# Stream cross products on four column groups, with three places for u blocks coming in and two going out

## The reference

```python
att = jnp.einsum('bhld,bhmd->bhlm', q, k) * decay
o = (jnp.einsum('bhlm,bhme->bhle', att, v)
     + jnp.einsum('bhld,bhde->bhle', q, S) * jnp.exp(lg[:, None] * (n + 1.0))[:, :, None])
kw = k * jnp.exp(lg[:, None] * (L - 1.0 - n))[:, :, None]
S_new = jnp.exp(lg * L)[:, None, None] * S + jnp.einsum('bhmd,bhme->bhde', kw, v)
...
x += W_o( sig(g_a) * ConvBranch(h) + sig(g_b) * RetentionBranch(h) ),  h = RMSNorm(x)
x += PEER(RMSNorm(x));   y = RMSNorm_final(x)
```

## Time and profile before

| | |
|---|---|
| three runs | 2183.03, 2184.49, 2186.46 us; median 2184.49 |
| the profiled execution | 2185.89 us, its span 2184.1 us |
| TensorE busy | 2139.8 us (98%) |
| VectorE busy | 1746.6 us (80%) |
| ScalarE, GpSimd busy | 619.3 us (28%), 860.8 us (39%) |
| DMA, mean over the span | 335 GB/s |

### The profile page before, as it was taken

The page is one execution under the profiler, slowest core; times in us unless marked ns, Lnnn a source line. Parts: engine busy times, 40 slices in busy tenths (PEclk is TensorE's granted clock), DMA queues, the critical chain, the costliest instruction groups (busy, mean ns, idle before and its releaser), DMA issues.

```text
span 2184.1 us, 31103 instructions
## 1 busy us (share of the span) xinstructions
PE 2139.8 (98%) x10569; PEld 1706.0 (78%) x10569; DVE 1746.6 (80%) x3270; ACT 619.3 (28%) x1197; POOL 860.8 (39%) x606
## 2 busy tenths in 40 slices
PE   6999999999999999999999999999999999999997
PEld 6999989999998985655565565677767888888886
DVE  2577586676765286898989979999969999999998
ACT  4212213132223111121211211233324444443434
POOL 4222122223333004475685675411145444444440
PEclk9999999999999999999999999999999999999999
DMA  5999999989983458999999999888999999999995
GB/s 191 300 329 308 300 299 330 333 299 326 305 287 136 137 195 336 336 372 412 397 410 412 383 412 412 299 290 298 301 340 411 414 414 413 414 414 414 414 415 202
DMA packets 312713, 732.28 MB, mean 335 GB/s; under 512 B 30208, under 2 KB 162048, under 8 KB 312576
## 3 DMA queue, kind: packets, MB, share of 16 engines
q1 hardware_dynamic: 188352, 436.52, 55.4%
q0 software_dynamic: 73728, 268.47, 31.3%
q10 hardware_dynamic: 50496, 25.59, 3.9%
HBM read 602.46 MB, written 128.00 MB: 334 GB/s over the span
## 4 chain that ended last, share of the span: by engine, by line
PE 61%; DMA 16%; DVE 14%; issue 4%; SPq 2%; ACT 1%; POOL 0%; DVEq 0%; ACTq 0%
PE ps L1833 29%; DMA b<-acts 12%; PE ps L1793 6%; PE ps L1596 6%; PE ps L1595 6%; PE ps L1594 6%; DMA b<-in_u_t 4%; PE ps L1848 4%; DVE b L1463 3%; DVE b L1509 2%; DVE b L1446 1%; DVE b L1515 1%; DVE b L1500 1%; SPq L527 1%; DVE b L1103 1%
## 5 line engine op out<-in xcount | busy, mean ns | idle before, releaser
L1833 PE MATMUL ps<-b,b 128*128 128x384 f32 x2048 | 665.6, 486 | 0.0
L732 POOL DMA_INDIRECT b<-u_rows,b x256 | 362.6, 1416 | 677.9 <-DVE b L1446 489.1
L1833 PEld LDWEIGHTS ps<-b,b 128*128 128x128 f32 x2048 | 386.8, 190 | 263.4
L695 POOL TENSOR_TENSOR b<-b,b 128x1024 fp32r<-128x1024 f32 x80 | 196.8, 2463 | 468.6 <-ACT b L745 464.0
L1463 DVE SCALAR_TENSOR_TENSOR b<-b,b,b 128x1024 f32<-128x1024 f32 x256 | 330.8, 1292 | 49.0 <-ACT b L966 32.6
L1594 PE MATMUL ps<-b,b 128*128 128x320 f32 x1152 | 364.5, 316 | 0.0
L1595 PE MATMUL ps<-b,b 128*128 128x320 f32 x1152 | 357.0, 310 | 0.0
L1596 PE MATMUL ps<-b,b 128*128 128x320 f32 x1152 | 357.0, 310 | 0.0
L732 POOL DMA_INDIRECT b<-in_peer_v,b x256 | 288.8, 1128 | 118.1 <-issue 76.9
L1446 DVE CUSTOM_DVE_ANT_0 b<-b,b 128x1024 f32<-128x1024 f32 x256 | 312.5, 1221 | 25.3 <-DMA b<-u_rows,b 23.8
L1103 DVE STREAM_TRANSPOSE b<-b 128x1024 f32<-128x1024 f32 x128 | 158.0, 1241 | 186.5 <-DMA b<-in_u_t 178.7
(11 more groups left out here) (164 smaller groups left out, 2414.0 us busy)
## 6 DMA issues: line engine op xcount, KB each, us to landing
b<-in_u_t SPq DMA_DIRECT2D x256, 512.0 KB, 6.5
u_rows<-b SPq DMA_DIRECT2D x512, 128.0 KB, 4.4
b<-in_peer_v SPq DMA_DIRECT2D x128, 512.0 KB, 22.1
b<-in_w_in SPq DMA_DIRECT2D x72, 512.0 KB, 6.4
b<-in_wq SPq DMA_DIRECT2D x48, 512.0 KB, 4.4
gates<-b ACTq DMA_DIRECT2D x12, 2048.0 KB, 8.3
b<-gates SPq DMA_DIRECT2D x32, 768.0 KB, 17.4
acts<-b SPq DMA_DIRECT2D x120, 192.0 KB, 7.9
```

The costliest lines, as they stand in the source:

```text
L695: nc.gpsimd.tensor_tensor(lo[u][:, :], raw[:, u, :], hi[u][:, :].bitcast(F32), ALU.subtract).then_inc(lo_ready, 1)
L732: nc.gpsimd.indirect_dma_start(slots[n % SLOTS][:, :], None, u_rows if kind == "u" else v_rows, bass.IndirectOffsetOnAxis(ap=row_id[:, r_ ...
L1833: last = nc.tensor.matmul(ps[:, up_bank(e), 0:TD], w[:, k * P:(k + 1) * P], h2[:, k, SD:T], start=(k == 0), stop=(k == KT - 1))
```

## The change

The cross products of all streams of a head are made in one block (`cross`), right behind the prompt's state at t = 4. The decayed q is now the stationary operand, 32 columns (two streams) at a time, and the state moves through it, 256 columns. The four pairs of streams write to four groups of 32 partitions of half a bank. `qg` is made twice, with zeros where the other stream of the pair stands (`own`), so that the second stream's product adds to the first's. The result has rows for frames; ScalarE copies it (`crow`), and at the end of t = 6 TensorE turns it by a product with the identity that adds to the streams' own attention (`stream_outputs`). ScalarE's root no longer waits for the last stream's state and is taken in two parts.

The places for u blocks are three in and two out, so `turn_in(m)` waits for block m - 3 to be turned, and `turn(m)` for block m - 2 to be stored. The ten turns behind the states of streams 1 to 7 are dealt out as 1, 2, 2, 2, 2, 1, 0 instead of 1, 1, 2, 1, 2, 1, 2; in the last head those behind streams 2 to 7 are 2, 2, 2, 1, 2, 1 instead of 2, 1, 2, 1, 2, 2. Left out below are two places that wait for all stores, now counted over two places.

```diff
--- before.py
+++ after.py
@@ -86,6 +86,7 @@
 TURN_IN = (2, 0, 2, 3, 4, 1, 3, 3)
 PER_HEAD = sum(TURN_IN)
 PER_CONV = 6
+TURNED_BEHIND_STREAM = (1, 2, 2, 2, 2, 1, 0)
 TURNED_GB = 2 + PER_HEAD
 TURNED_CONV = HEADS * PER_HEAD + TURNED_GB
 N_CONV = (NKEY - TURNED_CONV) // PER_CONV
@@ -182,7 +183,8 @@
     l = np.arange(P)[None, :]
     same = (l // STEP == m // STEP) & (l >= m)
     dec_s = np.stack([np.where(same, np.exp(g * np.maximum(l - m, 0)), 0.0) * scale for g in lg], 1)
-    gq = np.stack([np.broadcast_to(np.exp(g * (l % STEP + 1)), (P, P)) for g in lg], 1)
+    own = np.stack([l // STEP % 2 == a for a in range(2)], 1)
+    gq = np.stack([np.broadcast_to(np.exp(g * (l % STEP + 1))[:, None, :] * own, (P, 2, P)) for g in lg], 1)
     kcol = np.zeros((P, HEADS, PT + STREAMS))
     for h, g in enumerate(lg):
         for j in range(PT):
@@ -260,8 +262,8 @@
         wa_lo = [take(base, [P, D], F32R) for _ in range(GROUP)]
         ident = take(base, [P, P], F32)
         ones = take(base, [P, P], F32)
-        u_in = [x[:, i, :] for i in range(2)]
-        u_turned = [x[:, 2 + i, :] for i in range(3)]
+        u_in = [x[:, i, :] for i in range(3)]
+        u_turned = [x[:, 3 + i, :] for i in range(2)]
         g1 = take(base, [P, KT], F32)
         g2 = take(base, [P, KT], F32)
         ss = take(base, [P, TT], F32)
@@ -283,7 +285,7 @@
         sin = take(r, [P, T], F32)
         dec = take(r, [P, PROMPT], F32)
         dec_s = take(r, [P, P], F32)
-        gq = take(r, [P, P], F32)
+        gq = take(r, [P, 2 * P], F32)
         kcol = take(r, [P, HEADS, PT + STREAMS], F32)
         g16 = take(r, [P, HEADS], F32)
         kv = take(r, [P, TT, DK + DV], F32)
@@ -295,7 +297,8 @@
         att_at = [0, 512, 896, 1152, 1280]
         att_n = [512, 384, 256, 128, 128]
 
-        qg = [kv[:, 0, i * P:(i + 1) * P] for i in range(2)]
+        qg = [[kv[:, a, d * P:(d + 1) * P] for d in range(2)] for a in range(2)]
+        crow = att[:, 0:DV]
         sq = [att[:, i * T:(i + 1) * T] for i in range(2)]
         xs = at(conv_from, [P, 2, D], F32)
         hf = at(conv_from + 8192, [P, 2, 512], F32)
@@ -427,7 +430,9 @@
         st_stored = [sem(f"stream_state_stored{i}") for i in range(STREAMS)]
         s_loaded = [sem(f"s_loaded{i}") for i in range(STREAMS)]
         qg_ready = sem("qg_ready")
-        cross_done = sem("cross_done")
+        cross_done = sem("cross_rows_done")
+        crow_ready = sem("cross_rows_ready")
+        streams_done = sem("streams_done")
         sq_ready = sem("sq_ready")
         ms_done = sem("ms_done")
         orms_ready = sem("orms_ready")
@@ -464,9 +469,9 @@
         p_high = sem("p_high_done")
         p_split = sem("p_low_done")
         rows_ready = sem("row_numbers_ready")
-        u_loaded = [sem(f"u_tile_loaded{i}") for i in range(2)]
+        u_loaded = [sem(f"u_tile_loaded{i}") for i in range(3)]
         turned = sem("u_tile_turned")
-        u_stored = [sem(f"u_rows_stored{i}") for i in range(3)]
+        u_stored = [sem(f"u_rows_stored{i}") for i in range(2)]
         gelu_done = sem("row_gelu_only_done")
         hrow_done = sem("h_rows_done")
         hrow_ready = sem("h_rows_ready")
@@ -521,16 +526,16 @@
             def turn_out(m, r=0, per=0):
 
                 sp.wait_ge(turned, r * per + (m + 1))
-                src = u_turned[m % 3].rearrange("p (n f) -> p n f", n=4)
+                src = u_turned[m % 2].rearrange("p (n f) -> p n f", n=4)
                 for b in range(4):
                     dst = u_rows_of[ds(r * per + m, 1), b, :, :, :].rearrange("o i n f -> (o i) n f")
-                    sp.dma_start(dst, src[32 * b:32 * b + 32, :, :]).then_inc(u_stored[m % 3], 16)
+                    sp.dma_start(dst, src[32 * b:32 * b + 32, :, :]).then_inc(u_stored[m % 2], 16)
 
             def turn_in(m, r=0, per=0, first=False):
 
-                if not (first and m < 2):
-                    sp.wait_ge(turned, r * per + (m - 1))
-                sp.dma_start(u_in[m % 2], tile_of(io["u_t"], r * per + m)).then_inc(u_loaded[m % 2], 16)
+                if not (first and m < 3):
+                    sp.wait_ge(turned, r * per + (m - 2))
+                sp.dma_start(u_in[m % 3], tile_of(io["u_t"], r * per + m)).then_inc(u_loaded[m % 3], 16)
                 if not (first and m < 2):
                     turn_out(m - 2, r, per)
 
@@ -574,7 +579,7 @@
                         if not first:
 
                             sp.wait_ge(qg_ready, h * 2 - 2)
-                        for dst, n, w in ((dec, "dec", PROMPT), (dec_s, "dec_s", P), (gq, "gq", P)):
+                        for dst, n, w in ((dec, "dec", PROMPT), (dec_s, "dec_s", P), (gq, "gq", 2 * P)):
                             sp.dma_start(dst[:, :], io[n][:, ds(h * w - w, w)]).then_inc(tabs_loaded, 16)
                     if not first:
                         states_out(h - 2, STATES.get(t, ()))
@@ -812,9 +817,12 @@
                     for et in range(2):
                         act.wait_ge(o_done, g * 2 + (et + 1))
                         nc.scalar.activation(o_sb[:, et, 0:PROMPT], ps[:, 6 - 2 * et, :], ACT.Copy).then_inc(o_ready, 1)
+                if t == 5:
+                    act.wait_ge(cross_done, g + 1)
+                    nc.scalar.activation(crow, ps[:, 5, DV:2 * DV], ACT.Copy).then_inc(crow_ready, 1)
                 if t == 7:
 
-                    act.wait_ge(cross_done, g * STREAMS + STREAMS)
+                    act.wait_ge(streams_done, g + 1)
                     for et in range(2):
                         nc.scalar.activation(o_sb[:, et, PROMPT:T], ps[:, 7 - 2 * et, 0:P], ACT.Copy).then_inc(o_ready, 1)
                     act.wait_ge(o_ready, g * 4 + 4)
@@ -823,9 +831,11 @@
 
             def retention_end(g):
 
-                act.wait_ge(st_ready, g * 9 + 9)
                 act.wait_ge(ms_done, g + 1)
-                nc.scalar.activation(two(sq[0]), ps[:, 5:8:2, 0:HALF], ACT.Sqrt, bias=eps[:, 0:1]).then_inc(orms_ready, 1)
+                for hv in range(2):
+                    last = nc.scalar.activation(sq[0][:, hv * HALF:(hv + 1) * HALF], ps[:, 5 + 2 * hv, 0:HALF], ACT.Sqrt,
+                                                bias=eps[:, 0:1])
+                last.then_inc(orms_ready, 1)
 
             def head_tile(h, t, first=False, second=False):
 
@@ -1097,11 +1107,11 @@
             def turn(m, n, r=0, per=0):
 
                 for i in range(m, m + n):
-                    dve.wait_ge(u_loaded[i % 2], r * (per // 2 * 16) + 16 * (i // 2 + 1))
-                    if i >= 3 or per:
-                        dve.wait_ge(u_stored[i % 3], r * (per // 3 * 64) + 64 * (i // 3))
-                    nc.vector.transpose(u_turned[i % 3].rearrange("p (n k j) -> p n k j", n=4, k=KT),
-                                        u_in[i % 2].rearrange("p (k n i) -> p n k i", k=KT, n=4)).then_inc(turned, 1)
+                    dve.wait_ge(u_loaded[i % 3], r * (per // 3 * 16) + 16 * (i // 3 + 1))
+                    if i >= 2 or per:
+                        dve.wait_ge(u_stored[i % 2], r * (per // 2 * 64) + 64 * (i // 2))
+                    nc.vector.transpose(u_turned[i % 2].rearrange("p (n k j) -> p n k j", n=4, k=KT),
+                                        u_in[i % 3].rearrange("p (k n i) -> p n k i", k=KT, n=4)).then_inc(turned, 1)
 
             def rotate_q(h):
                 dve.wait_ge(evac, h * 8 + 2)
@@ -1128,9 +1138,10 @@
                     turn(16, 2)
                 for s in range(KW - PT):
                     stream_keys(g, s)
-                for i in range(2):
-                    then(nc.vector.tensor_tensor(qg[i], qT[:, i, PROMPT:T], gq[:, :], ALU.mult),
-                         qg_ready, g * 2 + (i + 1))
+                for a in range(2):
+                    own = gq[:, a * P:(a + 1) * P].unsqueeze(1).broadcast_to([P, 2, P])
+                    then(nc.vector.tensor_tensor(kv[:, a, 0:DK].rearrange("p (d l) -> p d l", d=2), qT[:, :, PROMPT:T],
+                                                 own, ALU.mult), qg_ready, g * 2 + (a + 1))
                 turn(0, 2, r, PER_HEAD)
 
             def key_decay(g, s):
@@ -1204,7 +1215,7 @@
                 done = 4
                 for s in range(1, STREAMS):
                     stream_state(g, s)
-                    n = 2 if s in (3, 5, 7) else 1
+                    n = TURNED_BEHIND_STREAM[s - 1]
                     turn(done, n, h, PER_HEAD)
                     done += n
                 outputs(g, lambda: turn(14, 2, h, PER_HEAD))
@@ -1235,7 +1246,7 @@
             done = n_gb + 6
             for s in range(2, STREAMS):
                 stream_state(HEADS - 1, s)
-                n = 2 if s in (2, 4, 6, 7) else 1
+                n = 2 if s < STREAMS - 1 and s != 5 else 1
                 turn(done, n)
                 done += n
                 if s == 4:
@@ -1665,15 +1676,31 @@
                                             start=(d == 0), stop=(d == 1))
                 last.then_inc(att_done, 1)
 
```

(47 more changed lines are left out.)

## The result

The changed kernel takes 2203.09 us (median of five runs, 2196.65 to 2205.68), the kernel before 2184.49: a ratio of 1.0083, 95% interval 1.0071 to 1.0096, 18.6 us. The profiled execution took 2203.09 us, its span is 2201.3 us against 2184.1. In the changed kernel L1657 is L1668, L1168 is L1179, L1103 is L1113, L1158 is L1169, L1683 is L1710, L1740 is L1764, L1673 has become L1688, the product lines L1594 to L1596 are L1605 to L1607, and SyncE's L527, L533, L578 are L532, L538, L583. In kernels with the cross products changed but the old order of turns in the middle heads, each of these numbers from L1113 on is one lower. L1614 is the product with `w_out` in the kernel before.

The account below looks back on a forecast made before the run. VectorE's u turns and their DMAs were taken to bound heads 1 to 3, TensorE just behind. Terms -6 + 1 + 1.9 + 2 = -1.1 gave 2184.8 us profiled, 2183.4 as median; range 2168 to 2195.

Parts of the forecast that it names:

- What bounds the kernel: Heads 1 to 3: set by VectorE's u turns and their DMAs, TensorE less than one us behind in two of three.
- The cross products: TensorE in each head: four column groups at once take 1.8 us, so work changes by -4.2 us (other end +1.2).
- the absorption in the heads: First three heads: the saving by itself gains nothing, since TensorE would wait the 4.2 us more for VectorE's copy of sums.
- Rival C: Cross products in each head: column groups do not work at once, 7.2 us in one block, +14, 2198 us; chance 0.12.
- a gain there has to be VectorE's: Conv stage, product with w_out: TensorE can come 1.9 us sooner than VectorE does, and no more.
- The u places: u blocks in the heads: one load per head issued early saves 1.5 us, -6 us over four heads.
- The ring's 0.3 per pair: u turns in the heads: the last store lands at +6.3 us, the load at +6.0, 0.3 us per pair of turns.
- The order: Turns ahead of stream states: stream 5's state comes later; in the last head TensorE enters the conv stage 1.9 us later.
- The wait named for the middle heads: TensorE before stream 7, waiting for stream 5's state: some 6 us idle per head, covered by slack in the first three heads.
- The clock: TensorE in the last head: idling before stream 7 drops it to the lower clock, +2 us (0 to 2.5).
- The eight states: Cross products in each head: TensorE waits some 3 us for all eight states, out of idle time it has anyway; taken as 0.
- D: Heads: stores cost 0.3 to 1.3 us per pair, late states lower the last head's clock; +4 to +9, 2191 us; chance 0.14.

Follow-up runs that it names:

- The pair with light loads: Kernel before and cross products alone, both loading only the first 256 of 1024 columns of each u block: 2175.73 us (0.9966) and 2158.33 us (0.9891).
- the kernel with those heads' half: Cross products with the new order of turns in the three middle heads only, places as before, against the kernel before: 2194.31 us, 1.0046.
- The kernel with early states: Cross products alone with the eight state loads issued behind the first, not the last, turn_in of t = 7, against the kernel before: 2193.45 us, 1.0046.

## Why the prediction was wrong, step by step

**What bounds the kernel** was right: VectorE's u turns and their DMAs set heads 1 to 3, and TensorE stands just behind. The pair with light loads shows it: the same edit is worth 17.4 us without that chain and less than nothing with it.

**The cross products**: the column groups, -4.2 us of work per head (4.35 us of time with light loads) and the absorption in the heads held. The estimate from the Trainium skill (TensorE: Matmul & The Clock Gate, section Measured speedup vs the span model) was 2.3 us for the block; the trace has 1.93, closer to a perfect share. Rival C fell with that row. Missed is the wait at the product with `w_out`, of which the prediction only said that a gain there has to be VectorE's; in the cross products alone it makes that product 5.8 us longer, where the sum had 0. The whole change does not have this wait. TensorE is held back elsewhere in it, and VectorE's last turn is 43.6 us ahead of the product.

**The u places** are the step that failed, with its sign: "I take 1.5 us less per head", -6 us in the sum, against a measured +11.6 alone and about +5 beside the other two parts. The ring's 0.3 per pair was near: 1.6 us more per ten turns are 0.4 per pair. Wrong was to credit the head with a load that is issued early, although the turn then waits for a store and not for a load. Also left out was what SyncE issues between a turn and its stores: the longest wait of 4.0 us became 5.9 alone and 6.7 in the change. That the place out is the scarce one is shown by two in, two out: 29 us slower.

**The order**: the mechanism was right and its size in the last head too small. The prediction had the last head's state done at 442.2 us and TensorE 1.9 us later. With the cross products it was done at 446.9 and L1763 came 8.8 us later than with the old order. I took the next turn from the trace of before, at 440.44 us, but it has moved to 443.9 with the cross products alone: a mark of one part was used for the sum of all. The wait named for the middle heads ("some 6 us per head") came, as 4.9 to 5.9 us; that it is free because VectorE does not wait for it is doubtful, since the kernel with those heads' half is 5 us slower in the median than without, barely clear of the noise. **The clock** of +2 was 2.7 in the last head, and 2.8 with the order alone.

**The eight states**: waits of 0.2 to 2.9 us, taken as 0. The kernel with early states gained nothing, but also took away only 0.8 us of them, so the 0 is neither refuted nor shown.

**Rivals and range**: the case that came is D, late states with the store ring's price, at twice its size: "+4 to +9" against 18.6. It was priced as small terms side by side. Measured, the parts alone are +5.8, +11.6 and +13.3, 31 together, and the change +18.6. The wait at the product with `w_out` (5.8 us in the first) is not in the change, and neither is the wait for the root in the last; the remaining overlap is not traced. "If the last head's products end more than 5 us later, D is" right: they end 15.9 us later.

## What to carry to other kernels

When two rings share a set of buffers, write for each the whole way from freeing a place to using it again, with what stands ahead on the issuing queue; the slower one sets the pace, and what the other gains counts for less (the third place in gave 18 us, the place out that paid for it cost 29). A saving on an engine that arrives just behind another is worth nothing until that other is relieved, so try the edit once with the other's load made light. Take the marks for a second part of a change from a trace that has the first, and read the last stage by itself: there a stall has no slack behind it.

## What the runs showed of the hardware

- 32 fp32 products with 32 columns stationary and 256 moving, spread over four column groups, take 1.93 us; 16 of 128x128 stationary and 256 moving take 3.61 us. The 32 at that price would be 7.2 us, so four groups give 3.7 times. After an idle 2.9 us in the second head the same 32 took 2.99 us.
- With three quarters of the bytes of the u loads gone, the kernel before is only 6.9 us faster (2175.73 against 2182.63): TensorE then has no wait for the copy of sums left, and its work sets the time.
- The same code up to the last head gave marks up to 9 us apart in two executions on two chips (the third copy of sums at 365.71 and 374.78 us), with the DMA engines over 90% busy: single marks say less than medians.
- VectorE's multiply of 128x640 took 0.83 us at 648.88 in the kernel before and 2.82 us at 677.33, where GpSimd's splits ran without a gap (667.14 to 679.5).
